# A hybrid GDN, conformer and mixture-of-experts block: the gain moved to the rows of x, the beta and decay products moved into the prologue

## The reference

```python
n1 = x * rsqrt(mean(x*x) + EPS) * g_mix
qkv, z, b_raw, a_raw, glu_in = split(n1 @ w_in)
beta = sigmoid(b_raw)
g = -exp(a_log) * softplus(a_raw + dt_bias)
u = glu_in + b_glu; u = u[:, :512] * sigmoid(u[:, 512:])
c = causal_depthwise_conv(u, w_conv_dw) + b_conv_dw
y_conv = silu(layernorm(c, ln_conv_g, ln_conv_b))
# q, k, v: causal conv of width 4, silu; then the gated delta rule with beta, g
# then w_out, a mixture of 64 experts, a gated embedding and a final norm
```

## Time and profile before

| | us |
|---|---|
| median of 3 runs | 1458.98 (1456.02 to 1459.46) |
| the profiled execution | 1454.21 |
| its span, first to last instruction | 1451.7 |
| prologue, until the last DVE operation ends | 0 to 35.2 |
| projection on PE | 36.2 to 300.1 |
| beta and decay products on PE | 300.1 to 323.1 |
| layer norm and decays | 323.7 to 363.6 |

### The profile page before, as it was taken

One profiled execution on the slowest core, in us unless ns is written; L12 is line 12 of the kernel. 1 busy time (PEld: TensorE's weight loads), 2 busy tenths in 40 slices (PEclk: granted clock), 3 DMA queues, 4 the chain that ended last, 5 costly groups with the idle time before them and its releaser, 6 DMA issues. The chain is left out here.

```text
span 1451.7 us, 16363 instructions
## 1 busy us (share of the span) xinstructions
PE 1186.1 (82%) x5812; PEld 794.6 (55%) x5812; DVE 629.5 (43%) x859; ACT 319.5 (22%) x667; POOL 242.1 (17%) x340
## 2 busy tenths in 40 slices
PE   4999999998588778899319878888887888748997
PEld 3888888885478677688303333333333332216775
DVE  7398989874465464532561111111111111144553
ACT  5121221214445333422101100010010010033222
POOL 2100000003535552000011111111112111111111
PEclk7999999967799899899659999999999999968999
DMA  4212111100000010411557999999799999962321
GB/s 147 59 44 58 43 46 44 40 1 0 0 1 1 1 59 1 152 74 73 225 241 312 424 428 424 424 414 396 292 424 427 427 420 415 418 225 78 113 94 43
DMA packets 68053, 272.59 MB, mean 188 GB/s; under 512 B 11625, under 2 KB 38442, under 8 KB 51370
## 3 DMA queue, kind: packets, MB, share of 16 engines
q1 hardware_dynamic: 56096, 254.30, 44.1%
q0 software_dynamic: 9456, 16.80, 3.0%
q10 hardware_dynamic: 2458, 0.92, 0.3%
HBM read 264.12 MB, written 25.43 MB: 199 GB/s over the span
## 5 line engine op out<-in xcount | busy, mean ns | idle before, releaser
L2110 PE MATMUL ps_u<-wup,xgT 128*64 128x512 f32 x1024 | 261.2, 669 | 62.8 <-DMA wup<-in_w_up_dram 60.4
L2110 PEld LDWEIGHTS ps_u<-wup,xgT 128*64 128x64 f32 x1024 | 86.7, 153 | 236.0 <-issue 234.8
L92 PE MATMUL ps_b<-n_hi,wh 128*128 128x512 f32 x384 | 150.7, 393 | 6.1 <-DVEq L405 6.1
L92 PE MATMUL ps_b<-n_lo,wh 128*128 128x512 f32 x384 | 150.4, 392 | 0.0
L92 PE MATMUL ps_b<-n_hi,wl 128*128 128x512 f32 x384 | 150.3, 391 | 0.0
L2030 DVE TENSOR_TENSOR hb<-sil,ps_u 128x256 f32<-128x256 f32 x32 | 13.4, 420 | 301.3 <-ACT sil L1967 301.3
L92 PEld LDWEIGHTS ps_b<-n_hi,wh 128*128 128x128 f32 x384 | 72.7, 189 | 21.6 <-ACTq L40 6.5
L92 PEld LDWEIGHTS ps_b<-n_lo,wh 128*128 128x128 f32 x384 | 72.8, 190 | 15.3
L92 PEld LDWEIGHTS ps_b<-n_hi,wl 128*128 128x128 f32 x384 | 72.7, 189 | 15.2
L423 DVE SCALAR_TENSOR_TENSOR convT<-upad,vecT,convT 128x1024 f32 (+1 forms) x60 | 76.7, 1278 | 0.0
L1967 ACT ACTIVATE sil<-ps_u 128x256 f32<-128x256 f32 x32 | 12.2, 383 | 288.9 <-PE ps_u L2110 288.9
(11 more groups left out here) (369 smaller groups left out, 2059.7 us busy)
## 6 DMA issues: line engine op xcount, KB each, us to landing
wup<-in_w_up_dram SPq DMA_DIRECT2D x64, 2048.0 KB, 17.7
zT<-in_w_down_dram SPq DMA_DIRECT2D x32, 1024.0 KB, 17.6
convT<-in_w_down_dram SPq DMA_DIRECT2D x32, 1024.0 KB
wraw<-in_w_in_dram SPq DMA_DIRECT2D x25, 512.0 KB, 4.0
convT<-y_rows SPq DMA_DIRECT2D x16, 512.0 KB, 5.2
qkvT<-in_x_dram SPq DMA_DIRECT2D x8, 512.0 KB, 7.4
qkvT<-in_w_out_dram SPq DMA_DIRECT2D x8, 512.0 KB, 5.0
xr<-in_x_dram SPq DMA_DIRECT2D x8, 512.0 KB, 3.2
```

The lines of the kernel that those rows point to most:

```text
L92: ins = nc.tensor.matmul(ps, lhs[a], rhs[b], start=first and k == 0, stop=last and k == 2)
L2110: last = nc.tensor.matmul(ps_u[k][HC[c], :], xgT[k][:, j, HC[c]], wup[k][c][:, j, :], start=j == 0, stop=j == NJ - 1)
```

## The change

Five edits go together:

- `g_mix` is loaded as 128 copies of a row (`gB1`), on ACT's queue, ahead of its seven small loads. DVE multiplies by it while it scales the rows of x (`scalar_tensor_tensor`), so `gained` and `tmp` are gone; `high` and `low` read PSUM.
- The eight columns for beta and decay are loaded by themselves (`wbr`), split in the prologue, and multiplied tile by tile on PE between the transposes (`gates`). The seventh weight load and split of the last iteration go, and the iteration is written out on ACT.
- The small operations that make beta and g stand at the head of the projection's ACT and DVE lists, ahead of the credits. `a_log` and `dt_bias` are loaded in the prologue.
- In the layer norm DVE adds the four channel groups of squares (`total`) and PE sums one group for each tile, in two halves (`variance`).
- `gc` is PE's first product in that block.

```diff
-        gmix = sb("gmix", [P, NJ])
...
-                    if t == 1:
-                        sp.dma_start(gmix[:], g_mix[0].rearrange("(p j) -> p j", j=NJ)).then_inc(s_loaded, 16)
+                    if t == 2:
+                        sp.dma_start(wbr, w_in_p[:, :, BAOFF:GOFF]).then_inc(s_wba, 16)
+                    if t == 3:
                         sp.dma_start(wraw[0][:], w_in_p[:, :, GOFF:GOFF + P]).then_inc(s_w[0], 16)
                 sp.dma_start(wraw[1][:], w_in_p[:, :, GOFF + CF:GOFF + CF + P]).then_inc(s_w[1], 16)
+                sp.dma_start(alog[:], a_log.partition_broadcast(P)).then_inc(s_dec, 16)
+                sp.dma_start(dtb[:], dt_bias.partition_broadcast(P)).then_inc(s_dec, 16)
...
+                act.dma_start(gB1, g_mix.partition_broadcast(P)).then_inc(s_loaded, 16)
...
-                    act.wait_ge(*v_norm.sem_at(f"tmp{t}"))
-                    nc.scalar.activation(n1[0][:, :, t * P:(t + 1) * P], tmp[t % 2], ACT.Copy).then_inc(*a_norm(f"hi{t}"))
+                    act.wait_ge(*p_norm.sem_at(f"T{t}"))
+                    nc.scalar.activation(n1[0][:, :, t * P:(t + 1) * P], ps_x[t % 2][:], ACT.Copy).then_inc(*a_norm(f"hi{t}"))
...
+                    if t == 2:
+                        act.wait_ge(s_wba, 16)
+                        nc.scalar.activation(wba[:, :, 0:2 * H], wbr, ACT.Copy).then_inc(*a_norm("b_hi"))
...
-                    if t >= 2:
-                        dve.wait_ge(*p_norm.sem_at(f"T{t - 2}"))
-                    nc.vector.tensor_scalar(xn[t % 2], xs[:, t, :], rs[:, t:t + 1], None, ALU.mult).then_inc(*v_norm(f"xn{t}"))
-
-                def gained(t):
-                    dve.wait_ge(*p_norm.sem_at(f"T{t}"))
                     if t == 0:
                         dve.wait_ge(s_loaded, 16)
                     if t >= 2:
-                        dve.wait_ge(*v_norm.sem_at(f"lo{t - 2}"))
-                    nc.vector.tensor_tensor(tmp[t % 2], ps_x[t % 2][:], gmix[:].unsqueeze(2).to_broadcast([P, NJ, P]),
-                                            ALU.mult).then_inc(*v_norm(f"tmp{t}"))
+                        dve.wait_ge(*p_norm.sem_at(f"T{t - 2}"))
+                    nc.vector.scalar_tensor_tensor(xn[t % 2], xs[:, t, :], rs[:, t:t + 1], gB1, ALU.mult, ALU.mult).then_inc(*v_norm(f"xn{t}"))
 
                 def low(t):
                     dve.wait_ge(*a_norm.sem_at(f"hi{t}"))
-                    nc.vector.tensor_tensor(n1[1][:, :, t * P:(t + 1) * P], tmp[t % 2],
+                    nc.vector.tensor_tensor(n1[1][:, :, t * P:(t + 1) * P], ps_x[t % 2][:],
                                             n1[0][:, :, t * P:(t + 1) * P].bitcast(F32), ALU.subtract).then_inc(*v_norm(f"lo{t}"))
 
-
                 scaled(0)
-                for t in range(NT + 1):
+                for t in range(NT):
                     if t + 1 < NT:
                         scaled(t + 1)
-                    if t < NT:
-                        gained(t)
-                    if t:
-                        low(t - 1)
-                dve.wait_ge(*a_norm.sem_at("w_hi"))
-                nc.vector.tensor_tensor(wl[0][:], wraw[0][:], wh[0][:].bitcast(F32), ALU.subtract).then_inc(*v_norm("w_lo"))
+                    low(t)
+                    if t == 2:
+                        dve.wait_ge(*a_norm.sem_at("b_hi"))
+                        nc.vector.tensor_tensor(wba[:, :, 2 * H:4 * H], wbr, wba[:, :, 0:2 * H].bitcast(F32),
+                                                ALU.subtract).then_inc(*v_norm("b_lo"))
+                    if t == 6:
+                        dve.wait_ge(*a_norm.sem_at("w_hi"))
+                        nc.vector.tensor_tensor(wl[0][:], wraw[0][:], wh[0][:].bitcast(F32), ALU.subtract).then_inc(*v_norm("w_lo"))
...
+                def gates(t):
+                    pe.wait_ge(*v_norm.sem_at(f"lo{t}" if t > 2 else "b_lo"))
+                    tok = slice(t * P, (t + 1) * P)
+                    nc.tensor.matmul(ps_ba[:, t, :], n1[0][:, 0, tok], wba[:, 0, :], start=True, stop=False)
+                    for j in range(NJ):
+                        nc.tensor.matmul(ps_ba[:, t, 0:2 * H], n1[1][:, j, tok], wba[:, j, 0:2 * H], start=False, stop=False)
+                    for j in range(1, NJ):
+                        last = nc.tensor.matmul(ps_ba[:, t, :], n1[0][:, j, tok], wba[:, j, :], start=False, stop=j == NJ - 1)
+                    last.then_inc(*p_norm(f"ba{t}"))
+
                 for t in range(NT):
                     pe.wait_ge(*v_norm.sem_at(f"xn{t}"))
                     if t >= 2:
-                        pe.wait_ge(*v_norm.sem_at(f"tmp{t - 2}"))
+                        pe.wait_ge(*v_norm.sem_at(f"lo{t - 2}"))
                     for j in range(NJ):
                         last = nc.tensor.transpose(ps_x[t % 2][:, j, :], xn[t % 2][:, j:D:NJ], ident[:])
                     last.then_inc(*p_norm(f"T{t}"))
+                    if t == 1:
+                        pe.wait_ge(s_vec, 7 * 16)
+                        nc.tensor.transpose(ps_v[:, 0:KC * NC_], vrow[0:KC * NC_, 0, :], ident[0:KC * NC_, 0:KC * NC_])
+                        nc.tensor.transpose(ps_v[:, P:P + RV], vrow[0:RV, 1, :], ident[0:RV, 0:RV]).then_inc(*p_norm("vecs"))
+                    if t >= 2:
+                        gates(t - 2)
+                gates(NT - 2)
+                gates(NT - 1)
...
+                nc.scalar.activation(ba[:], ps_ba[:, :, 2 * H:4 * H], ACT.Copy).then_inc(*a_gate("ba"))
+                act.wait_ge(s_dec, 32)
+                nc.scalar.activation(ea[:], alog[:], ACT.Exp).then_inc(*a_gate("ea"))
+                act.wait_ge(*v_gate.sem_at("ba"))
+                nc.scalar.activation(sm["eb"][:], ba[:, :, 0:H], ACT.Exp, scale=-1.0).then_inc(*a_gate("eb"))
+                act.wait_ge(*v_gate.sem_at("ay"))
+                nc.scalar.activation(sm["ey"][:], sm["ay"][:], ACT.Exp, scale=-1.0).then_inc(*a_gate("ey"))
+                act.wait_ge(*a_gate.sem_at("ey"))
+                nc.scalar.activation(sm["ln"][:], sm["ey"][:], ACT.Ln, bias=1.0).then_inc(*a_gate("ln"))
...
+                dve.wait_ge(*a_gate.sem_at("ba"))
+                nc.vector.tensor_tensor(ba[:], ba[:], ps_ba[:, :, 0:2 * H], ALU.add).then_inc(*v_gate("ba"))
+                dve.wait_ge(*v_gate.sem_at("ba"))
+                dve.wait_ge(s_dec, 32)
+                nc.vector.tensor_tensor(sm["y"][:], ba[:, :, H:2 * H], dtb[:].unsqueeze(1).to_broadcast(hb), ALU.add).then_inc(*v_gate("y"))
+                dve.wait_ge(*v_gate.sem_at("y"))
+                nc.vector.scalar_tensor_tensor(sm["ay"][:], sm["y"][:], -1.0, sm["y"][:], ALU.mult, ALU.max).then_inc(*v_gate("ay"))
...
+                dve.wait_ge(*a_gate.sem_at("ln"))
+                dve.wait_ge(*a_gate.sem_at("ea"))
+                dve.wait_ge(*v_gate.sem_at("ry"))
+                nc.vector.tensor_tensor(sm["y"][:], sm["y"][:], sm["ln"][:], ALU.add).then_inc(*v_gate("sp"))
+                dve.wait_ge(*v_gate.sem_at("sp"))
+                nc.vector.scalar_tensor_tensor(gdec[:], sm["y"][:], -1.0, ea[:].unsqueeze(1).to_broadcast(hb),
+                                               ALU.mult, ALU.mult).then_inc(*v_gate("g"))
...
-                        if n:
+                        if n == 3 and last:
+                            dve.wait_ge(*v_proj.sem_at(f"tap{cuts[n] - 1}", i))
+                            dve.sem_inc(*v_proj("lo6"))
+                        elif n:
                             low(n + 3, i, f"lo{n + 3}")
-                        if last and n == 3:
-                            dve.wait_ge(*v_proj.sem_at("lo6", i))
-                            nc.vector.tensor_copy(wba[:, :, 0:2 * H], wh[0][:, :, 0:2 * H].bitcast(F32))
-                            nc.vector.tensor_copy(wba[:, :, 2 * H:4 * H], wl[0][:, :, 0:2 * H].bitcast(F32)).then_inc(s_wba, 1)
...
-                pe.wait_ge(s_wba, 1)
-                for t in range(NT):
-                    tok = slice(t * P, (t + 1) * P)
...
-                last.then_inc(s_ba, 1)
...
+                nc.tensor.matmul(ps_m[:], tri[:], flat(gdec), start=True, stop=True).then_inc(*p_pre("gc"))
...
+                def variance(h):
+                    pe.wait_ge(*v_pre.sem_at(f"sqs{h}"))
+                    for t in range(4 * h, 4 * h + 4):
+                        last = nc.tensor.matmul(ps_v[:, t:t + 1], sqs[:, t * P:(t + 1) * P], ones[:, 0:1], start=True, stop=True)
+                    last.then_inc(*p_pre(f"var{h}"))
+
                 for t in range(5):
                     sums(t)
-                for t in range(NT):
-                    if t % 4 == 0:
-                        pe.wait_ge(*a_pre.sem_at(f"sq{t // 4}"))
-                    for m in range(NC_):
-                        last = nc.tensor.matmul(ps_v[:, t:t + 1], sq[:, m, t * P:(t + 1) * P], ones[:, 0:1], start=m == 0, stop=m == NC_ - 1)
-                last.then_inc(*p_pre("var"))
-                for t in range(5, NT):
-                    sums(t)
+                variance(0)
+                sums(5)
```

(38 more changed lines are left out.)

96 lines of the change are left out of this document (39 added, 57 removed).

## The result

The change takes 1469.89 us, median of 8 runs (1463.54 to 1472.42); the kernel before took 1458.36 in 8 runs on the same chip. The ratio is 1.0083, 95% interval 1.0062 to 1.0104: **9 to 15 us slower**. Forecast were 1470.0 us, within 1461 to 1475, and "slower" at 0.82. The profiled execution has a span of 1469.6 us (before 1451.7).

A forecast was written before the change was run, and what follows sets the result against it. DVE's round was taken to bound the prologue, with PE at half clock the bound after the change. Terms +19.6, +2.8, -6.7 and -4.6 sum to +11.1 us, added to the median 1459.0: 1470 us, range 1461 to 1475.

The forecast's parts named there:

- end of the prologue: Prologue: PE becomes the bound at half clock with added products, ending at 54.8 us instead of 35.2, +19.6 us.
- first product behind it: Projection's start: PE's first product comes 3.8 us behind the prologue's end, where it was 0.98; +2.8 us.
- a total: Layer norm: DVE's sum over four channel groups of squares, priced at 3.8 us from a row with stepped reads.
- scaled variance behind its block's start: Layer norm: the scaled variance, ready 27 us after its block starts, where it was 32.
- length of the layer norm block: Layer norm: an earlier variance, followed by about 8.1 us to the last copy, makes this part 4.6 us shorter.
- head: Everything up to the second copy `vr`, near the end of what the change touches; the summed effect was +11.1 us.
- The chain: Projection's start: small operations for beta and g, ahead of DVE's credit, delay PE's first product; +2.8 us.
- The tail: Projection's end: PE's 23 us of products go, but DVE's convolutions are right behind, so only -6.7 us.
- four broadcast passes: Layer norm, behind the variance: PE, idle for so long, runs them at half clock, 0.85 us each, not 0.43.
- the full clock: Rival, prologue: PE keeps full clock, so the prologue costs 3.1 us and the change is faster, 1454 us; 9%.
- come and go: Rival, prologue: PE's clock is full for about half the stretch, some 8 us less, 1462 us; 9%.
- a total stayed far below 6.2 us: Rival, layer norm: if each total takes over 6.2 us, the variance is no earlier, giving 1475 us; 4%.

The follow-up runs named there:

- e1: The changed kernel run again unaltered, for a second profile: 1468.75 us, ratio 1.0090 to the kernel before.
- e10: The changed kernel run unaltered once more, for a third profile: 1462.41 us, one run.
- e2: The changed kernel with each beta and decay product in the prologue padded with zero columns to 128 columns: 1455.47 us, ratio 1.0001 to the kernel before.
- e3: The changed kernel with ACT's and DVE's starting credits given ahead of the chain of small operations: 1464.9 us, ratio 1.0061 to the kernel before.
- e9: The kernel before, unchanged, run again for a second profile: 1458.67 us, ratio 1.0000.
- e8: The changed kernel with products behind the projection in wide form, and totals as two row additions: 1437.99 us, ratio 0.9867 to the kernel before.

## Why the prediction was right

By its steps, in us, from the three profiles of the change (the first, e1, e10):

| step | forecast | measured |
|---|---|---|
| end of the prologue | 54.8 (+19.6) | 55.4, 54.7, 54.0 |
| first product behind it | 3.8 (+2.8) | 3.7 in each |
| first product to the end of DVE's convolutions | 280.8 (-6.7) | 280.2, 279.8, 279.7 (-7.3 to -7.8) |
| a total | 3.8 | 3.65 to 3.68 in each |
| scaled variance behind its block's start | 27.1 | 26.2, 27.6, 27.6 |
| length of the layer norm block | 35.3 (-4.6) | 33.2, 34.2, 34.1 (-5.7 to -6.7) |
| head | +11.1 | +8.9, +8.8, +7.9 |
| everything behind it, in the medians | 0 | about +3 (11.5 less 8.5), open |

**The prologue** went as priced. PE became the bound, at half clock, with 3.41 for a group and 1.6 for eight transposes. The Trainium skill (TensorE: Matmul & The Clock Gate, "Why this matters for your kernels") would have a TensorE without gaps at full clock. Here it ran 35 us without one at half (steps of 0.21), so being busy was not enough for these products; in e2, the same products padded, the rule's full clock came after all, from 31.66.

**The chain** cost 2.75; e3 took it away and got 2.8 to 3.0 back.

**The tail** gave what was forecast where it was looked for: the gap between the taps shrank by 2.6 (2.7 was put), and nothing follows the convolutions. The whole stretch is 0.6 to 1.1 shorter than forecast, and that lies at the other end of the projection. Its first products step 0.43 us until the clock is back and 0.23 after that; the sixteenth starts 6.24 us behind the first in the profile of before, and 5.42, 5.03 and 4.93 behind it in the three of the change. It was 5.78 in e9, the kernel before, so a part of this is chance, and the prediction had put nothing for it.

**Layer norm** is the term most mis-sized, by 1.1 to 2.1 us. What the three profiles share is the end of the block, here in the first:

```profile
369.35 2.46 PE L636 MATMUL ps_s<-GT,ones 128*128 128x512 f32 x4 [0.41 <-POOL GT L648]
...
371.15 1.30 ACT L670 ACTIVATE vr<-ps_s 128x512 f32<-128x512 f32 x2
```

and the block in e10:

```profile
344.73 2.48 DVE L686 SCALAR_TENSOR_TENSOR convT<-ps_s,convT 128x512 f32<-128x512 f32 x4 [7.37 <-PE ps_s L611]
...
364.92 0.17 DVE L708 TENSOR_SCALAR vt<-ps_var 128x8 f32<-128x8 f32 x1 [1.00 <-PE ps_var L624]
...
368.85 1.98 PE L636 MATMUL ps_s<-GT,ones 128*128 128x512 f32 x4 [0.64 <-POOL GT L648]
```

From the scaled variance to the end of the last copy it is 7.0 in the first profile (371.15 + 1.30 = 372.45), and 6.6 in e1 and e10, not 8.1. The prediction let PE be idle ahead of the four broadcast passes and put them at half clock, 3.4 us. But PE was busy with the sums `ps_E` until 0.4 to 0.6 us before, and the four took 2.46, 1.99 and 1.98. It had kept that case as an edge of its range. Ahead of the variance the profiles differ among themselves: DVE's first centring came 5.96 us after the block's start in the first, but 7.43 and 7.37 in e1 and e10, where the clock rises some 3 us later in the block (1.00 from about 343.0 in the first, from about 345.0 in e1, whose block starts 1.05 earlier) and PE's 16 sums of channels take 10.1 and 10.0 us instead of 8.6. So the scaled variance came 0.9 earlier than put in one profile and 0.5 later in two, which is the spread between executions of one program. The totals were right by the stepped row. The Trainium skill has this as well, on another page than the one weighed before (Advanced Engine Details and Errata, "Memory Cachelines"): a new line at each access costs. The trace agrees, 3.67 us with a step of 4 KB against 2.27 in a line; e8's additions, which read in a line, need 1.9.

So the sum for the head was 2.2 to 3.2 us too high, and the untouched stages, costed at nothing, added about 3. The mechanism held step by step, but the median's agreement to 0.1 us is luck: these two cancel. Of the rivals, the full clock did not occur (e2, where it came for the later part of the stretch, shows that it was worth 13 us and more), nor did it come and go (in e10 only the first nine products were faster, 1.33 us together and not 1.9), and a total stayed far below 6.2 us.
